# Output projection and second norm of a hybrid decoder step: the last two column chunks by token tile, the norm in three groups, two expert tiles multiplied in the same block

## What is computed

```python
h = h + concat(rmsnorm(o_fox), rmsnorm(o_dil)) @ w_out
x2 = rmsnorm(h)
q = (x2 @ w_query).reshape(tokens, 8, 256)
s1 = q[..., :128] @ k1.T ; s2 = q[..., 128:] @ k2.T      # 128 scores each
v1, i1 = top_k(s1, 16) ; v2, i2 = top_k(s2, 16)
top, pos = top_k(v1[..., :, None] + v2[..., None, :], 16) # 16 of 256 sums
g = softmax(top)
hid = u_tab[eidx] . x2
out = sum(g * gelu(hid) * v_tab[eidx])
y = rmsnorm(h + out)
```

## Time and profile before

| | us |
|---|---|
| median of 3 runs (1703.65 to 1705.79) | 1705.03 |
| the profiled execution | 1705.38 |
| its span, first to last instruction | 1703.8 |
| PE busy in it | 1623.8 (95%) |
| DVE busy | 1360.3 (80%) |
| ACT busy | 776.4 (46%) |
| POOL busy | 579.9 (34%) |

### The profile page before, as it was taken

One profiled execution on the slowest core, in us unless ns is written; L12 is line 12 of the kernel. 1 busy time (PEld: TensorE's weight loads), 2 busy tenths in 40 slices (PEclk: granted clock), 3 DMA queues, 4 the chain that ended last, 5 costly groups with the idle time before them and its releaser, 6 DMA issues.

```text
span 1703.8 us, 27739 instructions
## 1 busy us (share of the span) xinstructions
PE 1623.8 (95%) x9666; PEld 1461.8 (86%) x9666; DVE 1360.3 (80%) x3159; ACT 776.4 (46%) x1262; POOL 579.9 (34%) x513
## 2 busy tenths in 40 slices
PE   5999987797999999989999999999999999999997
PEld 4999744497999999989999999997888888888886
DVE  4224585354899999979999999997999999999996
ACT  4222374223434433367767777763333333333334
POOL 0000380002544534654334334433343333433320
PEclk9999997997999999999999999999999999999999
DMA  3342562712333423499999999999999999999991
GB/s 119 106 156 94 164 198 98 271 73 78 130 131 109 135 100 107 158 354 371 388 369 397 382 370 388 404 404 389 404 403 399 404 405 399 404 403 399 404 365 53
DMA packets 158620, 463.52 MB, mean 272 GB/s; under 512 B 18224, under 2 KB 64432, under 8 KB 154546
## 3 DMA queue, kind: packets, MB, share of 16 engines
q1 hardware_dynamic: 98930, 248.59, 39.7%
q0 software_dynamic: 50944, 178.96, 27.5%
q10 hardware_dynamic: 8640, 34.61, 5.0%
HBM read 406.12 MB, written 57.63 MB: 272 GB/s over the span
## 4 chain that ended last, share of the span: by engine, by line
PE 47%; DVE 21%; DMA 3%; issue 3%; ACT 1%; POOL 1%; another core or an unknown queue 0%; SPq 0%; DVEq 0%; ACTq 0%; POOLq 0%
PE va L230 10%; PE va L231 10%; PE va L232 10%; PE hp L230 4%; PE hp L231 4%; PE hp L232 4%; DVE gathered L1396 3%; DVE og L1901 3%; DVE ulo L1912 2%; PE ggp L1841 2%; DVE vw L1396 2%; DMA hidden_values<-gelu_out 1%; DVE sc L1606 1%; DVE oh L1900 1%; DVE X L1605 1%
## 5 line engine op out<-in xcount | busy, mean ns | idle before, releaser
L230 PE MATMUL hp<-mid_hi,uhi 128*128 128x384 f32 x1024 | 354.6, 346 | 9.1 <-issue 3.5
L231 PE MATMUL hp<-mid_lo,uhi 128*128 128x384 f32 x1024 | 345.2, 337 | 0.0
L232 PE MATMUL hp<-mid_hi,ulo 128*128 128x384 f32 x1024 | 343.8, 336 | 0.0
L230 PE MATMUL va<-vhi,ahi 128*128 128x512 f32 x768 | 299.7, 390 | 3.4 <-DVE hid L1396 2.7
L231 PE MATMUL va<-vlo,ahi 128*128 128x512 f32 x768 | 299.5, 390 | 0.0
L232 PE MATMUL va<-vhi,alo 128*128 128x512 f32 x768 | 299.4, 390 | 0.0
L1771 POOL DMA_INDIRECT gathered<-in_v_experts,eidx x160 | 175.0, 1094 | 311.6 <-DVE acc L2221 222.8
L1309 POOL TENSOR_TENSOR ulo<-uw,uhi 128x1024 fp32r<-128x1024 f32 x49 | 124.1, 2533 | 261.0 <-ACT uhi L1305 261.0
L230 PEld LDWEIGHTS hp<-mid_hi,uhi 128*128 128x128 f32 x1024 | 193.2, 189 | 14.5 <-issue 5.6
L232 PEld LDWEIGHTS hp<-mid_hi,ulo 128*128 128x128 f32 x1024 | 193.3, 189 | 0.0
L231 PEld LDWEIGHTS hp<-mid_lo,uhi 128*128 128x128 f32 x1024 | 193.1, 189 | 0.0
(11 more groups left out here) (314 smaller groups left out, 3413.1 us busy)
## 6 DMA issues: line engine op xcount, KB each, us to landing
uw<-in_u_experts SPq DMA_DIRECT2D x128, 512.0 KB
vw<-in_v_experts SPq DMA_DIRECT2D x68, 512.0 KB
more_v<-in_v_experts SPq DMA_DIRECT2D x60, 512.0 KB
gate_matrix<-gst ACTq DMA_DIRECT2D x12, 2048.0 KB
hidden_values<-gelu_out SPq DMA_DIRECT2D x72, 192.0 KB
hd_mid<-hidden_values SPq DMA_DIRECT2D x8, 1536.0 KB
gt_mid<-gate_matrix SPq DMA_DIRECT2D x8, 1536.0 KB
hd_freed<-hidden_values SPq DMA_DIRECT2D x7, 1536.0 KB
```

Source lines behind the costliest of these rows:

```text
L230: nc.tensor.matmul(out, a_hi, b_hi, start=first, stop=False)
L231: nc.tensor.matmul(out, a_hi, b_lo, start=False, stop=False)
L232: return nc.tensor.matmul(out, a_lo, b_hi, start=False, stop=last)
```

## The change

- The last two column chunks are not made one after the other for all tiles. `PRODUCTS` lists the 20 products: chunks 0 and 1 as before, then chunk 2 and chunk 3 for the first two tiles, then both chunks for each of the other tiles. The tiles come in the order `OUT_ORDER` = 1, 2, 3, 0, 4, so that `at` is a position and t = `OUT_ORDER[at]` a tile. A tile is complete after product 12, 13, 15, 17, 19.
- The norm has three groups: positions 0 and 1, position 2, positions 3 and 4. The turns of the first three positions stand behind products 15, 16 and 18.
- The hidden tiles 0 and 1 are multiplied in this block, tile 0 ahead of the last two turns and tile 1 behind them. Their splits go to ACT and POOL here. Their PSUM tiles `hp` are also the first two of the five `acc`.
- The low parts of the first two query weights go from DVE to POOL.
- In routing, hidden tiles 0 and 1 only pass through gelu ahead of the loop; all others move up by `EARLY` = 2, and the tail has 14 instead of 16. SP fetches two expert tiles ahead of its loop.

```diff
-        def pipelined_norm(sems, source, row_of, slot_tiles, gain, stat, root, rtmp, sq, tp, hi, lo):
+        def pipelined_norm(sems, source, row_of, order, gain, stat, root, rtmp, sq, tp, hi, lo, GROUPS=((0, 3), (3, TT))):
...
-            def statistics(act, arrived):
-                for g, (a, b) in enumerate(GROUPS):
-                    for t in range(a, b):
+            def statistics(act, arrived, groups=range(len(GROUPS))):
+                for g in groups:
+                    a, b = GROUPS[g]
+                    for at in range(a, b):
+                        t = order[at]
                         r = rows(t)
-                        arrived(t)
-                        if t == 0:
+                        arrived(at)
+                        if at == 0:
                             act.wait_ge(cleared, 1)
                         else:
-                            act.wait_ge(squared, t)
-                        nc.scalar.activation(sq[:r], source(t), ACT.Square, accum_out=stat[:r, t:t + 1]).then_inc(squared, 1)
+                            act.wait_ge(squared, at)
+                        nc.scalar.activation(sq[:r], source(t), ACT.Square, accum_out=stat[:r, at:at + 1]).then_inc(squared, 1)
                     act.wait_ge(meaned, g + 1)
                     nc.scalar.activation(root[:, a:b], stat[:, a:b], ACT.Sqrt).then_inc(rooted, 1)
 
-            def half_split_hi(act):
-                for n in range(HALVES):
-                    t, k0 = n // 2, n % 2 * 4
+            def half_split_hi(act, halves=range(HALVES)):
+                for n in halves:
+                    t, k0 = order[n // 2], n % 2 * 4
...
+            def row(dve, at):
+                t = order[at]
+                g = sum(at >= b for _, b in GROUPS)
                 dve.wait_ge(inverted, g + 1)
-                if t >= 2:
-                    dve.wait_ge(turned, 2 * (t - 1))
+                if at >= 2:
+                    dve.wait_ge(turned, 2 * (at - 1))
...
+        EARLY, hidden = 2, ExitStack()
+        hp = [ps(hidden, f"hp{i}", [P, SEQ]) for i in range(2)]
+        ge_stored = [sem(f"ge_stored{i}") for i in range(2)]
+        u_hi, u_lo, h_mm, gelu_done = (sem(n) for n in ("u_hi", "u_lo", "h_mm", "gelu_done"))
...
-            acc = [ps(st, f"po_acc{t}", [P, 2, CW]) for t in range(TT)]
+            acc = [hp[i][:].rearrange("p (a n) -> p a n", a=2) for i in range(2)] + [ps(st, f"po_acc{t}", [P, 2, CW]) for t in range(2, TT)]
+            OUT_ORDER = (1, 2, 3, 0, 4)
+            PRODUCTS = [(c, at) for c in range(2) for at in range(TT)] + [(2, 0), (2, 1), (3, 0), (3, 1)] + [(c, at) for at in range(2, TT) for c in (2, 3)]
+            COMPLETE = [PRODUCTS.index((3, at)) for at in range(TT)]
...
+            norm = pipelined_norm(f_sems, source, row_of, OUT_ORDER, gain, stat, root, rtmp, sq, tp, x2hi, x2lo,
+                                  ((0, 2), (2, 3), (3, TT)))
...
+                act.sem_inc(gelu_done, 2)
+                for m in range(EARLY):
+                    u_split_hi(act, m, m, m)
+
+                def arrived(at):
+                    act.wait_ge(out_done, COMPLETE[at] + 1)
+
+                norm["statistics"](act, arrived, range(1))
+                norm["split_hi"](act, range(2))
+                norm["statistics"](act, arrived, range(1, 2))
+                norm["split_hi"](act, range(2, 6))
+                norm["statistics"](act, arrived, range(2, 3))
+                norm["split_hi"](act, range(6, 2 * TT))
+
+            @block.gpsimd
+            def _(pool):
+                for u in range(2):
+                    pool.wait_ge(q_split, u + 1)
+                    nc.gpsimd.tensor_tensor(q_lo[:, u], w_q[:, u], q_hi[:, u].bitcast(F32), ALU.subtract)
+                pool.sem_inc(u_lo, 2)
+                for m in range(EARLY):
+                    u_split_lo(pool, m, m, m)
...
-                for chunk in range(CHUNKS - 1):
-                    for t in range(TT):
-                        if t == 2 and chunk >= 1:
-                            split(chunk + 1)
-                        add_to_h(chunk, t)
-                add_to_h(CHUNKS - 1, 0)
-                for u in range(2):
-                    dve.wait_ge(q_split, u + 1)
-                    nc.vector.tensor_tensor(q_lo[:, u], w_q[:, u], q_hi[:, u].bitcast(F32), ALU.subtract)
-                add_to_h(CHUNKS - 1, 1)
-                add_to_h(CHUNKS - 1, 2)
+                for n in range(COMPLETE[1] + 1):
+                    if n in (7, 10):
+                        split(2 if n == 7 else 3)
+                    add_to_h(n)
                 norm["mean"](dve, 0)
-                add_to_h(CHUNKS - 1, 3)
                 norm["invert"](dve, 0)
                 dve.wait_ge(gain_ld, 16)
                 norm["row"](dve, 0)
-                add_to_h(CHUNKS - 1, 4)
+                add_to_h(14)
                 norm["row"](dve, 1)
-                norm["mean"](dve, 1)
-                norm["row"](dve, 2)
+                add_to_h(15)
                 norm["split_lo"](dve, 0)
                 norm["split_lo"](dve, 1)
+                norm["mean"](dve, 1)
                 norm["invert"](dve, 1)
-                for t in range(3, TT):
-                    norm["row"](dve, t)
-                    norm["split_lo"](dve, 2 * t - 4)
-                    norm["split_lo"](dve, 2 * t - 3)
-                for n in range(2 * TT - 4, 2 * TT):
+                add_to_h(16)
+                norm["row"](dve, 2)
+                norm["split_lo"](dve, 2)
+                norm["split_lo"](dve, 3)
+                add_to_h(17)
+                add_to_h(18)
+                norm["split_lo"](dve, 4)
+                norm["split_lo"](dve, 5)
+                add_to_h(19)
+                norm["mean"](dve, 2)
+                norm["invert"](dve, 2)
+                norm["row"](dve, 3)
+                norm["row"](dve, 4)
+                for n in range(6, 2 * TT):
                     norm["split_lo"](dve, n)
 
             @block.tensor
             def _(pe):
-                for chunk in range(CHUNKS):
-                    pe.wait_ge(lo_done, chunk + 1)
-                    for t in range(TT):
-                        cols = slice(t * P, t * P + rows(t))
-                        if chunk:
-                            pe.wait_ge(out_done, (chunk - 1) * TT + t + 1)
-                        for kind in range(2):
-                            for k in range(4 * kind, 4 * kind + 4):
-                                last = mm3(acc[t][:rows(t), kind], mid_hi[:, k, cols], mid_lo[:, k, cols],
-                                           whi[:, chunk % 2, k], wlo[:, chunk % 2, k], k == 4 * kind, k == 4 * kind + 3)
-                        last.then_inc(mm_done, 1)
-                norm["turn"](pe, range(TT))
+                pe.sem_inc(h_mm, 2)
+                for n, (chunk, at) in enumerate(PRODUCTS):
+                    t = OUT_ORDER[at]
+                    cols = slice(t * P, t * P + rows(t))
+                    if at == 0:
+                        pe.wait_ge(lo_done, chunk + 1)
+                    if n >= TT:
+                        pe.wait_ge(out_done, n - TT + 1)
+                    for kind in range(2):
+                        for k in range(4 * kind, 4 * kind + 4):
+                            last = mm3(acc[n % TT][:rows(t), kind], mid_hi[:, k, cols], mid_lo[:, k, cols],
+                                       whi[:, chunk % 2, k], wlo[:, chunk % 2, k], k == 4 * kind, k == 4 * kind + 3)
+                    last.then_inc(mm_done, 1)
+                    if n in (15, 16, 18):
+                        norm["turn"](pe, ((15, 16, 18).index(n),))
+                pe.wait_ge(out_done, 16)
+                pe.wait_ge(norm["hi"], 6)
+                pe.wait_ge(norm["lo"], 6)
+                hidden_product(pe, 0, 0)
+                norm["turn"](pe, (3, 4))
+                pe.wait_ge(out_done, 17)
+                hidden_product(pe, 1, 1)
...
+                for r in range(EARLY):
+                    u_fetch(sp, UR + r, r)
                 with sp.Fori(0, NH - 1) as j:
                     for u in range(2):
                         sp.wait_ge(qs["lo"], 2 * j + u + 3)
                         sp.dma_start(w[:, u], A["w_query"][2 * j + 2 + u]).then_inc(wld[u], 16)
                     for r in range(RT):
-                        u_fetch(sp, RT * j + UR + r, r % UR)
-                for e in range(MIX + UR):
+                        u_fetch(sp, RT * j + UR + EARLY + r, (EARLY + r) % UR)
+                for e in range(EARLY, MIX + UR):
...
-                u_split_hi(act, 0, 0, 0)
-                u_split_hi(act, 1, 1, 1)
+                for u in range(2):
+                    u_split_hi(act, EARLY + u, u, (EARLY + u) % UR)
+                    hidden_gelu(act, u, u)
                 with act.Fori(0, NH - 1) as j:
                     turn(j, False)
                 turn(NH - 1, True)
-                for e in range(QX):
+                for e in range(EARLY, QX):
...
```

(6 more changed lines are left out.)

102 lines of the change are left out of this document (45 added, 57 removed).

## The result

The changed kernel takes **1710.91 us** (median of 7 runs, 1708.57 to 1712.22); the kernel before, in the 7 runs shared with it, 1704.89 (1701.43 to 1705.79). The ratio is 1.0045, 95% interval 1.0034 to 1.0055: slower by 6.0 us by the medians, by 7.7 by the ratio. The forecast was 1703.9 with a range up to 1708.7, so the time lies outside the range, on the side of the rival "more collisions".

The account below looks back on a forecast made before the run. DVE's top-k chain was taken to bound routing. Block +0.7, clock -1.3, `eidx` -2.0, tail +1.5 and meetings 0 gave -1.1 us: 1704.3 for the profiled execution, 1703.9 us as median, range 1699.0 to 1708.7.

Parts of the forecast that it names:

- more collisions: Routing: the shifted split of `qwhi` meets more short DVE operations; two more meetings give 1708.5 us; chance 0.19.
- The block: Before routing: the block ends with PE at 401.7 where DVE ended at 400.98, +0.7 us; DVE ends near 399.
- The clock over the barrier: At the first query matmul: the slow clock loses 1.5 us instead of 2.8, so -1.3 us.
- the rival: Barrier before routing: the clock stays up across it, 1.5 us more are gained, 1702.4 us; chance 0.14.
- the comparison with the drop behind 1.97 us of waiting: Barrier: the clock went to 0.50 for some 3 us after a 1.97 us wait; the same was expected here.
- `eidx`: End of routing: POOL has nothing to split in DVE's last 4 us, so `eidx` takes about 0.45 us, -2.0 us.
- PE's wait for `sample_idx` and the tail: End of routing: PE stands 6.6 us, then tile 14 runs its first 3 us at the lower clock, +1.5 us.
- The sign of being wrong: Routing: the forecast is wrong if DVE's chain from `V` to `sample_idx` is not 291.3 +/- 2 us.
- The pattern of the meetings: Routing loop: `qwhi` and POOL's split start about 1.2 us earlier in seven turns; priced 0, ends two meetings of 2.3 us.
- The full worth of the tiles: Routing: if PE bounded it, 8.4 - 0.7 and the clock's 1.3 would be gained, 1696.0 us; chance 0.07.

Follow-up runs that it names:

- the one in two pieces: The changed kernel with each of POOL's splits in routing and the tail made as two instructions of half the columns; 1698.9 us, ratio 0.9963.
- The kernel with the loads back: The changed kernel with one 1-column Sqrt on ACT ahead of its loop, so table loads return to each turn; 1702.2 us, ratio 0.9981.
- the runs in which the chain was made shorter than PE's work: POOL's splits in four pieces: changed kernel 1700.4 us, before 1711.4, norm part alone 1707.8; in the loop only: changed 1692.1, before 1701.9.

## Why the prediction was wrong

*The block:* right. PE ends at 401.25, with the execution's 0.55 at 401.8 (401.7 forecast); DVE near 397.5 to 398 (399). One row was read low: product 19 ends at 386.45 + 0.28 = 386.73, not 386.56, worth less than 0.2 us.

*The clock over the barrier:* the forecast took half of the loss back (-1.3); the rival had it all, and in this execution the rival was right: the clock stays at 1.00, and from the first query matmul to the first `V` it is 25.1 us instead of 27.6, -2.5. What failed is the comparison with the drop behind 1.97 us of waiting, which one wait can't support: of the changed kernel's two waits of 1.97 us one brought the drop and one did not. It is luck in part. Of the seven profiled executions whose block has the two tiles, six kept the clock over the barrier, and the one in two pieces lost it for some 3 us.

*`eidx`:* right, 0.28 us (-2.2).

*PE's wait for `sample_idx` and the tail:* right in place and near in size: 6.26 us of waiting (6.6 forecast), then the clock at 0.50, +1.1 (+1.5 forecast). The kernel with the loads back has the same wait and 16.2 us from `I1` to the gates; with two pieces the wait is 0.84 us and the way 14.9. The sign of being wrong that came is the length of the chain: 297.5 us from the first `V` to the start of `sample_idx`, where 291.3 +/- 2 was given.

*The pattern of the meetings:* **this is the term that failed.** The forecast named the cause, the table loads that leave the loop and the half of `qwlo` that comes earlier, and priced it at 0 "for the sum, with two meetings fewer or more, 2.3 us each, as ends". The eight turns grew by 6.4 us in the profiled execution, nearly three meetings net. Two runs show that the loads set it: back in the changed kernel they give -8.7 us (between batches), out of the kernel before +7.1. That they do so through the split's position is read from the traces; the one run that moved the split alone missed its place. Two assumptions behind the bounds failed. A shifted split was treated as one independent meeting a turn, free to fall either way; but DVE's turn is a chain, so the 0.26 us by which the shifted split delayed it moved everything behind it under POOL's other splits, whose times are set by PE and didn't move: turn 0 got one meeting more, turn 1 got 4.8 us longer, turn 2 5.1 shorter. And the first hit could have been read from the trace of before: POOL's split at 22.3 less 1.2 us lands on the `ab` and `abf` instructions, 21.1 and 21.5 us behind the first `V`. The pattern behind it could not be had without following all eight turns.

*The sum with these sizes:* block +0.55, clock -2.5, chain +6.4 - 2.2, tail +1.1, later stages +0.4, less 0.55 for the earlier start, give the +3.2 us between the two profiled executions. The medians differ by 6.0. The rest isn't shown: only one execution of each was profiled, 0.5 us above its median before and 2.3 below it after. Single executions differ that much where nothing was changed: over the thirteen profiles the first product of the block comes at 327.8 to 333.9 us, and from the first product of the gate stage to the end it is 963.8 to 968.5.

*The full worth of the tiles:* rightly dismissed. In the runs in which the chain was made shorter than PE's work the tiles bring 7.4 us and the whole change 9.8 and 11.0; in the others nothing of it is seen (1702.2 us with the tiles and the loads, 1700.6 without the tiles).

The range ended 0.1 us above the fastest of the seven runs and 2.2 below the median. The mechanism of the slower rival was right and its size too small; whether its chance of 0.19 was too small, one outcome can't tell.

## What to carry to other kernels

Where two engines share a way to memory, the bound of a chain is in the phase between them: a change that only moves another engine's instruction by a microsecond can cost or gain more than the work it saves, so list the long instructions of the one against the short ones of the other before pricing the shift at 0. Cut the long instructions of the engine that has slack: four pieces of 0.7 us in place of one of 2.4 took 35 us off DVE's chain, and should stand only where the other engine's chain bounds the time. And what a moved piece of work is worth depends on what bounds the stage that it leaves: with PE as the bound the change gave 9.8 and 11.0 us, 7.4 of the latter by the two tiles, and with DVE as the bound it lost 6.
